# Prompt attention over 192 key columns instead of 256: two masked 64 x 64 quarters left out, values in half-shifted tiles, extra halves turned in pairs

## The reference

```python
def window_attention(q, k, v, dist, key_valid, sinks, rel_table):
    ...
    s = jnp.einsum('...qkgd,...skd->...kgqs', qg, k, preferred_element_type=jnp.float32)
    s = s * (hd ** -0.5) + rel_bias(dist, rel_table)
    mask = ((dist >= 0) & (dist <= WINDOW)) & key_valid[..., None, None, None, :]
    s = jnp.where(mask, s, -jnp.inf)
    sink = sinks.astype(jnp.float32).reshape(ATT_KV_HEADS, ATT_GROUP, 1, 1)
    m = jnp.maximum(jnp.max(s, axis=-1, keepdims=True), sink)
    p = jnp.exp(s - m)
    den = jnp.sum(p, axis=-1, keepdims=True) + jnp.exp(sink - m)
    o = jnp.einsum('...kgqs,...skd->...qkgd', (p / den).astype(v.dtype), v)
```

## Time and profile before

| what | value |
|---|---|
| median of 3 runs | 2295.7 us (2293.32 to 2296.13) |
| profiled execution, its own time | 2293.78 us |
| its span, first to last instruction | 2292.0 us |
| busy: TensorE, VectorE, ScalarE, GpSimd | 2272.5, 1325.5, 789.0, 499.5 us |
| attention blocks on TensorE | about 176 to 289 us |

### The profile page before, as it was taken

One profiled execution on the slowest core, in us unless ns is written; L12 is line 12 of the kernel. 1 busy time (PEld: TensorE's weight loads), 2 busy tenths in 40 slices (PEclk: granted clock), 3 DMA queues, 4 the chain that ended last, 5 costly groups with the idle time before them and its releaser, 6 DMA issues.

```text
span 2292.0 us, 39997 instructions
## 1 busy us (share of the span) xinstructions
PE 2272.5 (99%) x15517; PEld 2217.6 (97%) x15517; DVE 1325.5 (58%) x2081; ACT 789.0 (34%) x1608; POOL 499.5 (22%) x547
## 2 busy tenths in 40 slices
PE   8999999999999999999999999999999999999999
PEld 8996699999999999999999998899999999999999
DVE  6447734667667567575723324655766756757743
ACT  6458822423323323223410014523332332332312
POOL 1005600323323223220000003211331322322300
PEclk9999999999999999999999999999999999999999
DMA  8613030111111111121231126441111111111122
GB/s 229 87 38 99 11 105 1 56 54 40 46 55 46 46 55 37 55 71 49 97 77 38 37 84 178 145 153 34 47 47 56 43 48 55 37 55 55 37 65 76
DMA packets 181507, 151.29 MB, mean 66 GB/s; under 512 B 34861, under 2 KB 171017, under 8 KB 181244
## 3 DMA queue, kind: packets, MB, share of 16 engines
q1 hardware_dynamic: 178460, 137.06, 20.9%
q0 software_dynamic: 2720, 12.56, 1.8%
q10 hardware_dynamic: 224, 0.23, 0.0%
HBM read 126.76 MB, written 24.53 MB: 66 GB/s over the span
## 4 chain that ended last, share of the span: by engine, by line
PE 95%; ACT 2%; DVE 1%; DMA 1%; SPq 1%; issue 0%; POOL 0%; DVEq 0%; POOLq 0%
PE ps L2066 19%; PE ps L2063 19%; PE ps L2062 19%; PE ps L341 8%; PE ps L345 8%; PE ps L342 8%; PE ps L357 3%; PE ps L364 2%; ACT prob L1212 1%; PE ps L1108 1%; PE ps L1131 1%; DMA scratch_x<-x 1%; PE ps L2692 1%; PE ps L1530 1%; PE ps L1531 1%; PE ps L2673 1%
## 5 line engine op out<-in xcount | busy, mean ns | idle before, releaser
L2063 PE MATMUL ps<-h_lo,ring_hi 128*128 128x352 f32 (+2 forms) x1440 | 466.8, 325 | 0.0
L2062 PE MATMUL ps<-h_hi,ring_hi 128*128 128x352 f32 (+2 forms) x1440 | 466.5, 325 | 0.0
L2062 PE MATMUL ps<-f_hi,ring_hi 128*128 128x268 f32 (+1 forms) x1568 | 416.1, 285 | 0.0
L2063 PE MATMUL ps<-f_lo,ring_hi 128*128 128x268 f32 (+1 forms) x1568 | 415.7, 285 | 0.0
L1867 DVE TENSOR_TENSOR x<-x,ps 128x536 f32<-128x536 f32 (+1 forms) x392 | 277.7, 708 | 170.1 <-PE ps L2066 167.3
L2066 PE MATMUL ps<-f_hi,ring_lo 128*128 128x268 f32 (+1 forms) x1568 | 319.2, 285 | 0.0
L2066 PE MATMUL ps<-h_hi,ring_lo 128*128 128x352 f32 (+2 forms) x1440 | 313.1, 325 | 0.0
L2062 PEld LDWEIGHTS ps<-f_hi,ring_hi 128*128 128x128 f32 x1568 | 295.3, 188 | 0.0
L2063 PEld LDWEIGHTS ps<-f_lo,ring_hi 128*128 128x128 f32 x1568 | 294.9, 188 | 0.0
L2062 PEld LDWEIGHTS ps<-h_hi,ring_hi 128*128 128x128 f32 x1440 | 271.4, 188 | 0.0
L2063 PEld LDWEIGHTS ps<-h_lo,ring_hi 128*128 128x128 f32 x1440 | 271.1, 188 | 0.0
(11 more groups left out here) (383 smaller groups left out, 3508.9 us busy)
## 6 DMA issues: line engine op xcount, KB each, us to landing
ring_raw<-in_mlp_w_up SPq DMA_DIRECT2D x60, 512.0 KB, 4.1
ring_raw<-in_mlp_w_down SPq DMA_DIRECT2D x56, 512.0 KB, 3.4
raw<-in_mlstm_w_in SPq DMA_DIRECT2D x12, 1024.0 KB, 5.5
x<-scratch_x SPq DMA_DIRECT2D x8, 537.0 KB, 6.0
scratch_x<-x POOLq DMA_DIRECT2D x1, 4296.0 KB, 12.1
x<-scratch_x SPq DMA_DIRECT2D x8, 528.0 KB, 4.7
x_tok<-in_x_prompt SPq DMA_DIRECT2D x8, 512.0 KB, 7.7
raw<-in_attn_w_qkv SPq DMA_DIRECT2D x16, 256.0 KB, 6.6
```

The lines of the kernel that those rows point to most:

```text
L2062: nc.tensor.matmul(o, wh, hi[:, c], start=start, stop=False, skip_group_check=chained)
L2063: nc.tensor.matmul(o, wh, lo[:, c], start=False, stop=False, skip_group_check=chained)
```

## The change

Each full block keeps 192 score columns a head instead of 256. Every head has a main part of 128 x 128 (all 128 queries, and the keys from 64 before the block to 64 into it), and an edge part of 128 x 64: the upper 64 queries with the first 64 keys of the band, the lower 64 queries with its last 64. So:

- scores: four matmuls of 256 columns become four of 128 columns and eight of 64 x 64 (64 rows, 64-wide weights, 64 columns). In a first block (b = 1) the main part is made of three matmuls a head, one of them with a constant (`unseen`, -1e30) in place of keys, and four of the edge ones are with that constant too;
- softmax, exps and scaling go over 192 columns (in first blocks 192 too, where it was 144); the bias is laid out to match, and is read by sixteen DMAs;
- transposes: eight become six, four main ones and two in which the edges of two heads, which lie side by side, are turned together (therefore `head_of` orders heads so that k % 2 is the key head);
- probT copy: one of 768 columns instead of 1024;
- values: v tokens lie in tiles shifted by 64 (`turn_v`, with a tile 0 from a small copy that `v_edge_pool` makes on GpSimd), so two matmuls over 128 keys are left, and four edge matmuls of 64 keys with 64-wide weights and 2 x 64 columns are added. For half of these v must lie on the other 64 partitions: `v_cross` copies them there by DMA into `v_nat`. That lies where block 1's probabilities were, so the DMA waits for `t_done` 2, and block 1's values wait for the DMA.

The core of the diff:

```diff
+        def v_edge_pool(pool, half):
+            if half:
+                pool.wait_ge(vt_ready, 3)
+                pool.wait_ge(out_free, V_LAST + 1)
+            else:
+                pool.wait_ge(out_free, 1)
+            nc.gpsimd.tensor_copy(vT_0[:, 0:LAST], vT[:, COL_S:T])
+            nc.gpsimd.tensor_copy(vT_0[:, LAST:HD], vT[:, COL_M:T])
+            nc.gpsimd.tensor_copy(vT_0[:, HD:P], vT[:, 0:HD]).then_inc(pool_made, 1)
+        def v_rows(t):
+            return P if t < NBLK else HD
+        def turn_v(t, o):
+            n = v_rows(t)
+            src = vT_0[:, :] if t == 0 else vT[:, t * P - HD:t * P - HD + n]
+            return nc.tensor.transpose(o[0:n, :], src, ident)
...
+        def v_cross(sp, gp):
+            if gp == 0:
+                sp.wait_ge(v_taken, 3)
+                sp.wait_ge(t_done, 2)
+            else:
+                sp.wait_ge(v_taken, V_TAKEN)
+            sp.dma_start(v_nat[0:HD, gp, :, :], v_tok[HD:P, 0:NBLK, gp * P:gp * P + HD]).then_inc(att_in, 16)
+            sp.dma_start(v_nat[HD:P, gp, :, :], v_tok[0:HD, 1:NBLK + 1, gp * P + HD:gp * P + P]).then_inc(att_in, 16)
...
             for p0 in range(0, P, COPIES):
-                sp.dma_start(bias[p0:p0 + COPIES, :, :],
-                             line_src(BLK - 1 - p0, [[LINE - 1, COPIES], [BLK * LINE, QH], [1, 2 * BLK]])
-                             ).then_inc(bias_in, 16)
+                c0, e0, e_src = (0, 3 * HD, 0) if p0 < HD else (HD, 0, 3 * HD)
+                for to, src, w in ((c0, c0, 3 * HD), (e0, e_src, HD)):
+                    sp.dma_start(bias[p0:p0 + COPIES, :, to:to + w],
+                                 line_src(BLK - 1 - p0 + src, [[LINE - 1, COPIES], [BLK * LINE, QH], [1, w]])
+                                 ).then_inc(att_in, 16)
...
+        SEEN = BLK + HD
+        prob = [at(f"prob{i}", (R4, R4 + 4096, R5, R1 + 29216)[i], [P, 4 * SEEN]) for i in range(P_BUFS)]
+        probT = [at(f"probT{i}", o, [P, 6 * BLK]) for i, o in enumerate(
+            (WHI + 4096 * (10 % 4), WHI + 4096 * (11 % 4), WLO + 4096 * (11 % 4)))]
         prob_m = at("prob_m", R0 + 36768, [META, 4, META])
-        prob_1 = at("prob_1", WLO + 4096 * (10 % 4), [P, 4, 2 * BLK])
+        prob_1 = at("prob_1", WLO + 4096 * (10 % 4), [P, 4 * SEEN])
+        v_nat = at("v_nat", WLO + 4096 * (10 % 4), [P, 2, NBLK, HD])
+        unseen = at("unseen", R0 + 35232, [P, HD])
...
+        def main_at(k):
+            return HD * (k % 2)
+        def edge_at(k):
+            return BLK * (1 - k % 2)
+        def scores_of(n, k):
+            return ps[:, 2 * (n % 2) + k % 2, 2 * BLK * (k // 2):2 * BLK * (k // 2) + SEEN]
+        def bias_of(n, step, k):
+            h = head_of(step, k)
+            if n % TILES == 0:
+                return bias[0:META, h, BLK:BLK + META]
+            return bias[:, h, 0:SEEN] if k % 2 else bias[:, h, HD:HD + SEEN]
...
-            for i in range(2):
-                for par in range(2):
-                    rows = slice(HD * par, HD * par + HD)
-                    bank = 2 * (n % 2) + par
-                    lhsT = q[rows, 4 * gp + 2 * ip + i, qc:qc + nq]
-                    o = ps[0:nq, bank, 2 * BLK * i:2 * BLK * i + 2 * BLK]
-                    if npk == BLK:
-                        last = nc.tensor.matmul(o, lhsT, kn[rows, gp, pc:pc + 2 * BLK], start=True, stop=True)
-                    else:
-                        if npk:
-                            nc.tensor.matmul(o[:, k0:BLK], lhsT, kn[rows, gp, pc:pc + npk],
-                                             start=True, stop=True)
-                        last = nc.tensor.matmul(o[:, BLK:k1], lhsT, kn[rows, gp, qc:qc + nq],
-                                                start=True, stop=True)
+            for k in range(4):
+                rows = slice(HD * (k % 2), HD * (k % 2) + HD)
+                lhsT = q[rows, 4 * gp + 2 * ip + k // 2, qc:qc + nq]
+                if b == 0:
+                    last = nc.tensor.matmul(scores_of(n, k)[0:nq, 0:nq], lhsT, kn[rows, gp, qc:qc + nq],
+                                            start=True, stop=True)
+                    continue
+                o = scores_of(n, k)[:, main_at(k):main_at(k) + BLK]
+                if b == 1:
+                    nc.tensor.matmul(o[:, 0:HD - META], ones[rows, :], unseen[rows, 0:HD - META], start=True, stop=True)
+                    nc.tensor.matmul(o[:, HD - META:HD], lhsT, kn[rows, gp, COL_M:COL_M + META], start=True, stop=True)
+                    nc.tensor.matmul(o[:, HD:BLK], lhsT, kn[rows, gp, qc:qc + HD], start=True, stop=True)
+                else:
+                    nc.tensor.matmul(o, lhsT, kn[rows, gp, qc - HD:qc + HD], start=True, stop=True)
+            if b:
+                for half, kc in enumerate((qc - BLK, qc + HD)):
+                    for k in range(4):
+                        rows = slice(HD * (k % 2), HD * (k % 2) + HD)
+                        qs = slice(HD * half, HD * half + HD)
+                        o = scores_of(n, k)[qs, edge_at(k):edge_at(k) + HD]
+                        if kc < 0:
+                            nc.tensor.matmul(o, ones[rows, qs], unseen[rows, :], start=True, stop=True)
+                        else:
+                            last = nc.tensor.matmul(o, q[rows, 4 * gp + 2 * ip + k // 2, qc:qc + BLK][:, qs],
+                                                    kn[rows, gp, kc:kc + HD], start=True, stop=True)
             last.then_inc(s_done, 1)
...
+                    for k in range(4):
+                        rows = slice(HD * (k % 2), HD * (k % 2) + HD)
+                        qs = slice(HD * half, HD * half + HD)
+                        o = scores_of(n, k)[qs, edge_at(k):edge_at(k) + HD]
+                        if kc < 0:
+                            nc.tensor.matmul(o, ones[rows, qs], unseen[rows, :], start=True, stop=True)
+                        else:
+                            last = nc.tensor.matmul(o, q[rows, 4 * gp + 2 * ip + k // 2, qc:qc + BLK][:, qs],
+                                                    kn[rows, gp, kc:kc + HD], start=True, stop=True)
             last.then_inc(s_done, 1)
         def att_transpose_pe(pe, n):
-            (qc, nq), (pc, _, npk), k0, k1, step = block_of(n)
+            qc, nq, step, b = block_of(n)
             pe.wait_ge(prob_ready, n + 1)
             if n >= 1:
                 pe.wait_ge(pT_ready, n)
             for k in range(4):
-                bank = 4 + k // 2
-                for part, (c0, nk) in enumerate(((k0, npk), (BLK, nq))):
-                    if nk:
-                        o = ps[0:nk, bank, (k % 2) * 2 * BLK + part * BLK:][:, 0:nq]
-                        last = nc.tensor.transpose(o, prob_of(n, slice(0, nq), k, slice(c0, c0 + nk)),
-                                                   ident[0:nq, 0:nq])
+                pr = prob_of(n, k)
+                if b:
+                    pr = pr[:, main_at(k):main_at(k) + BLK]
+                last = nc.tensor.transpose(ps[0:nq, 4, BLK * k:BLK * k + nq], pr, ident[0:nq, 0:nq])
+            if b:
+                for i in range(2):
+                    e = 2 * SEEN * i + BLK
+                    last = nc.tensor.transpose(ps[:, 5, BLK * i:BLK * i + BLK], prob_all(n)[:, e:e + BLK], ident)
             last.then_inc(t_done, 1)
...
-            for part, (t, nk) in enumerate(((pt, npk), (b - 1 if b else None, nq))):
-                for par in range(2):
-                    cols = slice((2 * gp + par) * HD, (2 * gp + par) * HD + HD)
-                    o = ps[HD * par:HD * par + HD, 6 + n % 2, 0:2 * BLK].rearrange("p (i s) -> p i s", i=2)[:, :, 0:nq]
-                    v = v_tok[:, t, cols] if t is not None else v_meta[:, cols]
-                    if nk:
-                        last = nc.tensor.matmul(o, v, probT_of(n)[0:nk, 2 * par:2 * par + 2, part, 0:nq],
-                                                start=part == 0 or npk == 0, stop=part == 1)
+            if n in (1, 2 * TILES + 1):
+                pe.wait_ge(att_in, 16 * 16 + (32 if n == 1 else 64))
+            o = ps[:, 6 + n % 2, 0:2 * BLK].rearrange("p (i s) -> p i s", i=2)
+            own = probT_of(n)[:, 0:4 * BLK].rearrange("p (k s) -> p k s", k=4)
+            edge = probT_of(n)[:, 4 * BLK:6 * BLK].rearrange("p (i s) -> p i s", i=2)
+            for par in range(2):
+                rows = slice(HD * par, HD * par + HD)
+                cols = slice((2 * gp + par) * HD, (2 * gp + par) * HD + HD)
+                if b == 0:
+                    last = nc.tensor.matmul(o[rows, :, 0:nq], v_meta[:, cols], own[0:nq, par:4:2, 0:nq],
+                                            start=True, stop=True)
+                else:
+                    nc.tensor.matmul(o[rows, :, :], v_tok[:, b - 1, cols], own[:, par:4:2, :], start=True, stop=False)
+            if b:
+                for half in range(1 if b == 1 else 0, 2):
+                    for par in range(2):
```

(26 more changed lines are left out.)

123 lines of the change are left out of this document (65 added, 58 removed).

## The result

The changed kernel takes 2304.4 us, the median of five runs (2302.7 to 2306.3), against 2295.7: a ratio of 1.004, 95% interval 1.0026 to 1.0054. It is slower by 8.7 us, where 2303.5 was forecast. (The 2295.7 is itself the median of five runs, 2293.3 to 2296.1.) The number was right, and that was luck. The rest of this document shows that the reason for it was wrong: the ten microseconds are lost at 40 to 60 us, by an edit that neither the prediction nor the diff above it shows, and attention, where all of the forecast loss was put, is no slower than before. In two of the experiments one run (2454.6 and 7889.2 us) was far slower than the rest, and is left out of the median.

The account below looks back on a forecast made before the run. TensorE (5.87 us a pair of blocks) and ScalarE (5.94) were taken as nearly equal bounds in attention; TensorE rising to 6.48 a pair, plus first blocks, less absorbed idle, gave +8.3 us: 2303.5 us, range 2291 to 2313.

Parts of the forecast that it names:

- The sum, +8.3: Attention: TensorE +11.8 us over full and first blocks, less 3 us absorbed by idle time and 0.5 for shorter exps.
- What I cost at nothing: Start and side work: sixteen bias DMAs, later SP queue, seven small GpSimd copies and fills, all taken as covered.
- 0.44 for eight: Attention scores: a block's eight 64 x 64 edge matmuls take 0.44 us on TensorE, at most 0.92.
- what would make it outright wrong: Attention scores: edge pairs overlap across all four quarters of the array, so scores fall under 0.8 us a block.
- The changes of shape: Attention on TensorE: six more tile-shape changes per pair of blocks, 0.14 to 0.19 us each, 0.89 us a pair.
- Rival 1: Attention: changes between 64-row and 64 x 64 tiles are free; -5.5 us, 2290, faster; chance 14%.
- rival 4: Attention: shape changes cost only the wait, 0.09 to 0.10 us, and more idle is absorbed; +2 to +4 us, 2298; 14%.
- 3 us of TensorE's 4.7 us of idle time: Attention, 189 to 289 us: 3 us of the added TensorE work fills its 4.7 us of idle time.
- a first block's scores: First blocks' scores: twelve main matmuls 1.50 us for 1.00, eight edge ones 0.44, two new shape changes 0.33.
- Rival 2: Attention values: the edges' two diagonal quarters don't run side by side, 0.92 us for 0.46; +13.8 us, 2317; 11%.
- Rival 3: Block 1's values: the cross copy to v_nat lands late, at 199 us; kernel ends 5 to 10 us after forecast; 6%.
- The bias DMAs, SP's later queue and the GpSimd copies: Next weights and k_raw some 6 us later on SP, GpSimd copies 0.2 us each; all expected to be hidden.

Follow-up runs that it names:

- one-load kernel: The changed kernel with the sinks in one contiguous DMA of 64 bytes a partition, put in order by VectorE while negating: 2294.0 us, ratio 0.9999 to the kernel before.

## Why the prediction was right in its number, and why not in its reason

- **The sum, +8.3, was put in the wrong stage.** The step that failed is "What I cost at nothing". It goes through the DMAs and copies that the change adds, but not the sinks' eight loads for four; they cost 9.4 us, shown alone: 1024 more packets at 113 a microsecond, ahead of the store of x that the kn drain waits for. What I had put on the path, the attention, costs -0.35, nothing that can be told. That the two errors are nearly equal is luck.
- **The edge scores were mis-sized.** "0.44 for eight" is 0.23 to 0.26 (by how the price of a change is split), since all four quarters of the array work at once; I had two. The prediction named this as what would make it outright wrong: a block's scores stream 0.48 + 0.23 = 0.71 us (or 0.44 + 0.26), below its 0.8 if that is read without the changes (with them they take 1.05). That is 0.21 a block, 5.9 us over 28.
- **The changes of shape were right**: 0.14 to 0.19 us forecast; 0.17 in the scores and 0.15 in the values, shown by taking them away and by adding more. Rival 1 and the price of rival 4 (0.09 to 0.10) fall with it. Values of two blocks 2.33 us (2.3 forecast), transposes 0.80 (0.80), a first block's scores 2.15 in the one-load kernel (250.44 to 252.59; 2.27 by the forecast's terms), exps 443 ns and copy 804 ns as forecast.
- **More was absorbed.** I took 3 us of TensorE's 4.7 us of idle time; with one load all but 0.2 is filled, some 1.5 us more. In this rival 4 was right.
- Together: 8.3 - 5.9 - 1.5 - 0.5 (four first blocks, 0.12 each less) = +0.4, against the -0.35 measured. So these terms close to within what the runs can tell.
- **Rival 2** (diagonal quarters not side by side) did not happen. By the Trainium skill, page "TensorEngine Tiling (Array Packing)", section "Gotcha 1: PSUM Pressure", it should have; the values' edges take 0.58 us with their change, so 0.43 streamed, and 0.92 if the pairs had taken turns. **Rival 3** did not happen either: TensorE never waits for v_nat in the trace; its only longer wait near 190 us, 2.1 us, is for GpSimd's scaling, and the kernel before has it too (2.2).
- The bias DMAs, SP's later queue and the GpSimd copies stayed hidden, as the kernel with one load shows: all of them are in it.

## What to carry to other kernels

Read every line of a diff for the DMAs that it adds, those of a few bytes too: count their contiguous pieces where these have 4 or 8 bytes, not their DMAs or bytes, and look at what stands behind them in the queue. A forecast that hits the time isn't thereby shown; one run with the unpriced edit alone, and one without it, told here that wrong terms had met. And where an experiment frees the wait that a trace names and the time stays, the delay stands further up: follow it to the transfer.

## What the runs showed of the hardware

- **4- and 8-byte pieces.** 128 partitions x 16 values in 4-byte pieces, instead of 8 bytes at a time, are 1024 packets more, and the kernel is 9.4 us slower. In the steady stretch 113 packets go in a microsecond at either size, so 7 on each of 16 engines if they share evenly, 0.14 us a piece; yet the busy share recorded there is 0.05. The first few hundred go faster (514 packets from 31 to 32 us in the changed kernel). The 1024 pieces of 32 bytes of `wg_raw` pass far more quickly, nearly all of them in the one microsecond from 33 us of the one-load kernel:

```profile
DMA packets 1229, 0.21 MB, mean 207 GB/s; under 512 B 1087, under 2 KB 1229, under 8 KB 1229
```

  So among pieces of different sizes their number alone is no measure either. Whether it is the size below 32 bytes that makes the others slow, or that all partitions read the same few bytes of HBM, wasn't tried. The first 8 us had cover. SP was held meanwhile, at the DMA behind: 10.61 us for an issue that took 1.18. The Trainium skill, page "DMA: Bandwidth & Descriptors", section Specifications, gives 512 bytes as the least for line rate; no run here tests that figure, and it wouldn't have given this size, since the quick 32-byte pieces lie below it too.
- **Four quarters, out of order.** In a first block the edge scores are first all of the first half (L1170, masked columns), then all of the second (L1172). TensorE in order of time, one-load kernel:

```profile
252.11 0.27 PE L1170 MATMUL ps<-unseen,cst 64*64 64x64 f32 x2
252.14 0.27 PE L1172 MATMUL ps<-kn,q 64*64 64x64 f32 x2
252.22 0.23 PE L1170 MATMUL ps<-unseen,cst 64*64 64x64 f32 x2
252.25 0.22 PE L1172 MATMUL ps<-kn,q 64*64 64x64 f32 x2
```

  The second half starts 0.03 us behind the first, ahead of matmuls that precede it in the program. The Trainium skill, page "TensorE: Matmul & The Clock Gate", section "The mechanism", says that matmuls start and end strictly in program order; these records disagree on the start.
- **The clock.** In the changed kernel the granted clock is 0.66 on the mean of 50 to 60 us, so 1.2 GHz for a part of it and 2.4 for the rest, around and after the time that TensorE stood for the drains; with TensorE busy all through (one load) it is 1.00 there. The changed kernel's matmuls of 358 columns start 0.30 us apart from 53.8 us on, where they start 0.16 apart before the stall. So a part of what a stall costs can come behind it.
